# High and low parts of the weight blocks interleaved word by word

## What is computed

```python
h = rms_norm(x, norm2_g[i])
ff = jax.nn.silu(jnp.einsum('bsd,df->bsf', h, w_gate[i])) * jnp.einsum('bsd,df->bsf', h, w_up[i])
x = x + jnp.einsum('bsf,fd->bsd', ff, w_down[i])
```

## Time and profile before

| | |
|---|---|
| Median of 3 runs | 1372.46 us (1371.91 to 1372.87) |
| Span of the profiled execution, first to last instruction | 1369.8 us |
| TensorE busy | 1296.2 us, 95% of the span, 6025 matmuls |
| Weight loads of TensorE (they overlap the matmuls) | 1027.9 us, 75% |
| DVE / ACT / POOL busy | 584.7 / 507.0 / 566.8 us |
| Loaded from HBM | 110.03 MB |
| Matmuls' mean granted clock | 0.974 of full speed |

### The profile page before, as it was taken

The page is one execution under the profiler, slowest core; times in us unless marked ns, Lnnn a source line. Parts: engine busy times, 40 slices in busy tenths (PEclk is TensorE's granted clock), DMA queues, the critical chain, the costliest instruction groups (busy, mean ns, idle before and its releaser), DMA issues.

```text
span 1369.8 us, 15424 instructions
## 1 busy us (share of the span) xinstructions
PE 1296.2 (95%) x6025; PEld 1027.9 (75%) x6025; DVE 584.7 (43%) x841; ACT 507.0 (37%) x782; POOL 566.8 (41%) x429
## 2 busy tenths in 40 slices
PE   7987599999999999999999999889989999999997
PEld 5765587688888888888887865555668888888886
DVE  4983442434114511211385345456477513314223
ACT  5573332634222211221464435545354323224132
POOL 4331244255455554454554432211236444544540
PEclk9999799999999999999999999989999999999999
DMA  6422202232333333332332231101214333333321
GB/s 170 151 62 69 70 17 77 62 108 86 106 93 92 103 98 93 95 105 77 108 95 75 78 61 46 47 18 31 76 47 123 93 99 100 93 93 104 96 62 62
DMA packets 218367, 114.44 MB, mean 84 GB/s; under 512 B 21604, under 2 KB 216368, under 8 KB 218040
## 3 DMA queue, kind: packets, MB, share of 16 engines
q1 hardware_dynamic: 217192, 110.50, 28.4%
q10 hardware_dynamic: 976, 2.90, 0.6%
q0 software_dynamic: 128, 0.07, 0.0%
HBM read 110.03 MB, written 2.38 MB: 82 GB/s over the span
## 4 chain that ended last, share of the span: by engine, by line
PE 77%; DVE 4%; issue 3%; ACT 3%; POOL 3%; SPq 1%; DMA 0%; DVEq 0%; ACTq 0%; POOLq 0%
PE bank L1995 21%; PE bank L1997 21%; PE bank L1996 21%; POOL wl L1953 2%; PE bank L1146 1%; PE aux L1162 1%; PE aux L1075 1%; PE aux L1995 1%; PE bank L1024 1%; PE aux L1087 1%; PE bank L2043 1%; PE bank L1026 1%; PE bank L1025 1%; PE bank L2045 1%; PE bank L2044 1%
## 5 line engine op out<-in xcount | busy, mean ns | idle before, releaser
L1953 POOL TENSOR_TENSOR wl<-raw,wh 128x512 fp32r<-128x512 f32 (+1 forms) x402 | 543.5, 1375 | 739.3 <-ACT wh L2373 739.3
L1995 PE MATMUL bank<-ah,wh 128*128 128x512 f32 x888 | 354.8, 400 | 24.8 <-POOL wl L1953 23.7
L1996 PE MATMUL bank<-ah,wl 128*128 128x512 f32 x888 | 347.7, 392 | 0.0
L1997 PE MATMUL bank<-al,wh 128*128 128x512 f32 x888 | 347.6, 391 | 0.0
L2373 ACT CAST wh<-raw 128x1024 fp32r<-128x1024 f32 (+1 forms) x201 | 208.1, 1038 | 374.9 <-PE bank L1997 362.9
L1995 PEld LDWEIGHTS bank<-ah,wh 128*128 128x128 f32 x888 | 168.0, 189 | 65.9 <-POOL wl L1953 24.7
L1997 PEld LDWEIGHTS bank<-al,wh 128*128 128x128 f32 x888 | 167.8, 189 | 35.6
L1996 PEld LDWEIGHTS bank<-ah,wl 128*128 128x128 f32 x888 | 168.0, 189 | 35.3 <-issue 1.5
L1995 PE MATMUL bank<-yh,wh 128*128 128x512 f32 x488 | 190.7, 391 | 0.1
L1997 PE MATMUL bank<-yl,wh 128*128 128x512 f32 x488 | 190.0, 389 | 0.0
L1996 PE MATMUL bank<-yh,wl 128*128 128x512 f32 x488 | 189.9, 389 | 0.0
(11 more groups left out here) (451 smaller groups left out, 1556.5 us busy)
## 6 DMA issues: line engine op xcount, KB each, us to landing
raw<-in_w_up SPq DMA_DIRECT2D x54, 512.0 KB, 3.9
raw<-in_w_down SPq DMA_DIRECT2D x48, 512.0 KB, 3.9
raw<-in_w_in SPq DMA_DIRECT2D x39, 512.0 KB, 3.9
raw<-in_w_gate SPq DMA_DIRECT2D x22, 512.0 KB, 3.9
raw<-in_w_out SPq DMA_DIRECT2D x16, 512.0 KB, 3.6
raw<-in_ple_gate SPq DMA_DIRECT2D x8, 512.0 KB, 3.7
raw<-in_w_down SPq DMA_DIRECT2D x8, 384.0 KB, 3.3
xtok<-in_x SPq DMA_DIRECT2D x4, 512.0 KB, 5.2
```

The lines of the kernel that those rows point to most:

```text
L1953: nc.gpsimd.tensor_tensor(wl[pl.slot[b]][:, half], raw[b % RAW][:, half], wh[pl.slot[b]][:, half].bitcast(F32), ALU.subtract).then_inc(wl_ ...
L1995: nc.tensor.matmul(ps, h[:, c:c + P], mh[:, k, :], start=(n == 0), stop=False)
L1996: nc.tensor.matmul(ps, l[:, c:c + P], mh[:, k, :], start=False, stop=False)
L1997: last = nc.tensor.matmul(ps, h[:, c:c + P], ml[:, k, :], start=False, stop=(n == nk - 1))
```

## The change

The pair of tiles for a slot becomes one tile of 1024 x 2 words. The high part takes the even words, the low part the odd ones; `wh` and `wl` become lists of views with a step of two words. Sizes, start addresses and all instructions but for the steps in their access patterns stay.

```diff
-        wh = [sb(f"wh{i}", [P, WB], F32R) for i in range(SPLIT)]
-        wl = [sb(f"wl{i}", [P, WB], F32R) for i in range(SPLIT)]
+        halves_of = [sb(f"wh{i}", [P, WB, 2], F32R) for i in range(SPLIT)]
...
-        wh.append(sb("wh3", [P, WB], F32R))
-        wl.append(sb("wl3", [P, WB], F32R))
+        halves_of.append(sb("wh3", [P, WB, 2], F32R))
+        wh, wl = ([w[:, :, part] for w in halves_of] for part in range(2))
```

## The result

The changed kernel takes 1422.53 us (median of 4 runs, 1420.43 to 1424.51) against 1372.66 us before (a fourth run of the kernel before is in this median): ratio 1.0363, 95% interval 1.0345 to 1.0382. The forecast was no change, 1372.8 us within 1370 to 1388. It is 50 us off, and outside the range.

The account below looks back on a forecast made before the run. The prediction took TensorE, busy 95% of the span, to bound the kernel. Its terms, 0 + 0 + 0 + (0 to 1) us, gave 1372.46 + 0.3 = 1372.8 us, within 1370 to 1388.

Parts of the forecast that it names:

- Item 2: TensorE's streaming reads in the value projections: taken as no cost, bounded by half rate at +23 us; that case's chance 0.06.
- The upper bound of that item: Streaming reads in the value projections at half rate, 0.417 ns more a column, +23 us in all; chance 0.06.
- Item 1: TensorE's weight loads under 512-column products: taken as no cost, bounded by half rate, up to +55 us over 4128 products.
- even a good part of a doubling is hidden: Claim that a much longer weight load still fits under the 226.7 ns between starts of 512-column products, costing nothing.
- 107 to 115 ns of cover: Time to spare for a weight load of 111 or 120 ns hidden under 512-column products 226.7 ns apart.
- Items 3 and 4: ACT's writes of wh, taken as no cost (bound +6 us); POOL's subtractions, taken as 0 to 5% slower, up to +1 us.
- POOL pays: Rival: POOL's halves in the chain slow at the double step; wh input at half rate +10.4 us, 1383 us; chance 0.17.
- a rise of half: POOL's price one step further, at a byte step over 8, by the Trainium skill: the +10.4 us.
- Item 5: DVE and POOL slow each other already; less of it not expected, and DVE, at 43%, waits for TensorE in long stretches.
- That rival: Weight loads spill out from under the products: 0 to +55 us, +18 us at a load of 231 ns, 1390 us; chance 0.06.

Follow-up runs that it names:

- e7: Kernel computing nothing of the reference, executed once, measuring distances of starts by stream length and start; 128 columns: 110 ns at stationary step 1, 118 at step 2.

## Why the prediction was wrong

- **Item 2, the streaming side.** "I take nothing" failed. The upper bound of that item was the truth: 0.417 ns more a column, +23 us forecast for that case, +22.4 us measured alone (+22.5 in the starts of the changed kernel). The bound was computed and given 0.06. Its support was that the stream is the fastest reader, and that should have weighed more: the row for 256 columns showed a word every 0.417 ns, the fastest access in the kernel, and no row showed slack in it. The Trainium skill ("SBUF — State Buffer", the note on SBUF cachelines under Door 1) says two hits on a 16-byte line give full speed. The measurement differs for this stream: step 2 has two words of each line and runs at half rate, runs of two words as well. It took four words in a run to be nearly whole, and the measurement decides.
- **Item 1, the weight loads.** The step that failed is "even a good part of a doubling is hidden". The load did not double. It is 8 ns longer, by the row of 128 columns (110 to 118 ns) and by its record (189 to 197 ns), and that against 107 to 115 ns of cover. By the working of item 1 that costs nothing; it cost 6.6 ns on each of 4459 products, 29.4 of the +31.0 us (the rest is seven products more that fall into that kind). The count of item 1 was low as well: 4644 products of 512 columns have a block as the stationary side, not 4128. The fault is to take a load that ends before the next start as one that costs nothing. At step 1 it is 512 columns at 0.417 ns = 213.3 and 13.3 ns more, for 256 columns 106.7 and 13.3. The prediction used the difference of the two and never asked what the 13.3 ns are. The runs do not say either. With the step this rest is 20.0 ns at 512 columns; at step 1 it is no fixed cost, since it is 16.8 ns at 480 columns and 22.0 at 488 (216.8 and 225.3 ns), and at a granted clock of 0.50 (e7, 285.7 to 287.2 us) 512 columns start 427 ns apart, 512 x 0.833, with no rest. So what is shown is where the cost lies, each stepped load under 510 to 512 columns, and that the cover did not remove it; the mechanism stays open.
- **Items 3 and 4, ACT and POOL.** Right in the main. ACT +7.5% in the kernel (+6% alone), POOL +1%, both covered; TensorE's waits for POOL did not grow. The rival "POOL pays", the likeliest with 0.17, falls: at step 2 its price is 1.8% alone. The extra input was no guide, since reading it at step 2 costs 13 ns of 1262. For one step further the prediction had named a rise of half; at step 4 on input and output it is 21% (1522 ns).
- **Item 5, collisions.** Right: DVE's busy time is 584.7 and 584.4 us, and the shared tile alone costs nothing.
- **The range.** A cost came on both sides of TensorE at once, and the prediction let in only one at a time. Both at once were 1414 us by its prices (+23 and +18), at 0.06 x 0.06 if taken as independent. But they hang on one question, what the step costs where TensorE reads, and should have had a common chance and a common price. Even 1414 would have missed: the +18 us were for a load that doubles and spills out, and the loads cost +31 us without either. That rival named the right place for a reason that the runs do not bear out.

## What to carry to other kernels

Keep what TensorE reads in contiguous words: a stream of 4-byte words at any step from two to four runs at half rate, and a stationary tile at step 2 costs 6.6 ns a product under 512 columns even where its load is hidden. Bounds that depend on one unknown are one rival with the summed price. Cover by overlap is a claim to test on a row in which the covered part varies and the covering one stays; a rest in the distance of starts that the stream does not explain (13.3 ns here) is a sign that the two may not simply overlap.

## What was not expected of the hardware

- Streaming 512 four-byte columns: 227 ns at step 1, 450 at steps 2 and 3, 461 at step 4; step 3 is no dearer than step 2. In bf16, step 2 costs 4% (5.58 against 5.36 us for 24).
- Stationary loads of 128 columns where they bind: 110, 118, 176, 233 ns at steps 1 to 4. Here the step of two is nearly free and the step of four doubles. The last was taken at a granted clock of 0.50, and at 1.00 with 256 columns it is the same 233 to 234 ns.
- ACT's copy of 1024: 1044, 1105, 1549, 1988 ns at output steps 1 to 4. POOL's subtraction of 512: 1262, 1285, 1522 ns at steps 1, 2, 4.
- From 488 to 512 columns most distances of starts lie at 220.0, 226.7 or 233.3 ns, and a stream of 508 columns with a stepped load is as fast as 512 columns without the step.
